# Turning the adaLN blocks of the pair steps by transpositions, and making some of them two slots earlier

## The reference

```
mod = silu(c) @ w_ada + b_ada          # 9 conditioning rows (1 prompt, 8 samples), 6144 columns
shift1, scale1, gate1, shift2, scale2, gate2 = split(mod, 6)
h = rms_norm(x, g_norm1) * (1 + scale1) + shift1
qa, ka, va, qb, kb, vb, qi, ki, wi, fl, ga, gb = split(h @ w_in)
oa = sparse_attend(...)   # top 128 keys of the indexer's scores, ALiBi, QK-norm
ob = forget_attend(...)   # causal, with cumulative log forget values, QK-norm
x = x + gate1 * ((sigmoid(ga) * (oa @ w_o_a) + sigmoid(gb) * (ob @ w_o_b)) @ w_out)
h2 = rms_norm(x, g_norm2) * (1 + scale2) + shift2
x = x + gate2 * (square(relu(h2 @ w_up)) @ w_down)
```

## Time and profile before

| | us |
|---|---|
| median of 3 runs | 942.34 |
| lowest, highest | 941.03, 943.38 |
| the profiled execution | 939.24 |
| its span | 937.4 |
| TensorE busy in the span | 919.6 (98%) |
| VectorE busy | 493.9 (53%) |
| ScalarE busy | 396.2 (42%) |

### The profile page before, as it was taken

One profiled execution on the slowest core, in us unless ns is written; L12 is line 12 of the kernel. 1 busy time (PEld: TensorE's weight loads), 2 busy tenths in 40 slices (PEclk: granted clock), 3 DMA queues, 4 the chain that ended last, 5 costly groups with the idle time before them and its releaser, 6 DMA issues.

```text
span 937.4 us, 19878 instructions
## 1 busy us (share of the span) xinstructions
PE 919.6 (98%) x7554; PEld 847.5 (90%) x7554; DVE 493.9 (53%) x1178; ACT 396.2 (42%) x829; POOL 141.0 (15%) x140
## 2 busy tenths in 40 slices
PE   8999999999999999999999999999999999999997
PEld 7797678777878878998999999999999999999997
DVE  3654778864645797731277576444333344443332
ACT  3354646654756667233334244333111244431121
POOL 4200233232236674300000000000000000000000
PEclk9999999999999999999999999999999999999999
DMA  9648765256325554977233431233333333333312
GB/s 319 219 117 235 188 214 174 71 169 193 110 64 158 163 183 131 279 251 249 69 91 97 129 90 47 69 92 94 98 96 91 90 90 89 89 89 90 89 45 92
DMA packets 176233, 124.54 MB, mean 133 GB/s; under 512 B 14739, under 2 KB 152019, under 8 KB 176164
## 3 DMA queue, kind: packets, MB, share of 16 engines
q1 hardware_dynamic: 176034, 123.50, 43.6%
q10 hardware_dynamic: 130, 0.10, 0.0%
HBM read 116.99 MB, written 6.59 MB: 132 GB/s over the span
## 4 chain that ended last, share of the span: by engine, by line
PE 88%; DVE 5%; issue 4%; ACT 2%; POOL 1%; POOLq 0%; ACTq 0%; DVEq 0%
PE bank L976 24%; PE bank L977 23%; PE bank L978 23%; PE bank L1064 2%; PE bank L1087 2%; PE bank L1043 2%; PE bank L882 2%; PE bank L1073 2%; PE bank L1105 1%; PE bank L1261 1%; PE bank L900 1%; PE bank L1049 1%; PE bank L1128 1%; DVE sel L2027 1%; PE bank L1118 1%
## 5 line engine op out<-in xcount | busy, mean ns | idle before, releaser
L976 PE MATMUL bank<-h_hi,w_hi 128*128 128x256 f32 (+1 forms) x1232 | 357.5, 290 | 1.2 <-issue 0.6
L977 PE MATMUL bank<-h_lo,w_hi 128*128 128x256 f32 (+1 forms) x1232 | 348.0, 282 | 0.0
L978 PE MATMUL bank<-h_hi,w_lo 128*128 128x256 f32 (+1 forms) x1232 | 347.5, 282 | 0.0
L976 PEld LDWEIGHTS bank<-h_hi,w_hi 128*128 128x128 f32 x1232 | 232.3, 189 | 23.5 <-issue 17.0
L977 PEld LDWEIGHTS bank<-h_lo,w_hi 128*128 128x128 f32 x1232 | 232.1, 188 | 0.0
L978 PEld LDWEIGHTS bank<-h_hi,w_lo 128*128 128x128 f32 x1232 | 231.7, 188 | 0.0
L976 PE MATMUL bank<-u_hi,w_hi 128*128 128x264 f32 (+1 forms) x512 | 145.1, 283 | 0.0
L977 PE MATMUL bank<-u_lo,w_hi 128*128 128x264 f32 (+1 forms) x512 | 144.7, 283 | 0.0
L978 PE MATMUL bank<-u_hi,w_lo 128*128 128x264 f32 (+1 forms) x512 | 144.5, 282 | 0.0
L2444 DVE TENSOR_TENSOR w_lo<-raw,w_hi 128x1024 fp32r<-128x1024 f32 x58 | 71.1, 1225 | 132.9 <-ACT w_hi L1783 132.9
L1783 ACT ACTIVATE w_hi<-raw 128x1024 fp32r<-128x1024 f32 x58 | 61.3, 1056 | 139.8 <-PE bank L978 139.8
(11 more groups left out here) (330 smaller groups left out, 1372.2 us busy)
## 6 DMA issues: line engine op xcount, KB each, us to landing
raw<-in_w_in SPq DMA_DIRECT2D x44, 512.0 KB, 4.0
part<-in_w_ada SPq DMA_DIRECT2D x32, 512.0 KB, 5.5
raw<-in_w_up SPq DMA_DIRECT2D x32, 512.0 KB, 4.1
raw<-in_w_down SPq DMA_DIRECT2D x32, 512.0 KB, 4.0
ada<-in_w_ada SPq DMA_DIRECT2D x4, 2048.0 KB, 13.6
kv<-in_cache_k_b SPq DMA_DIRECT2D x16, 256.0 KB, 4.1
qbc<-q_d SPq DMA_DIRECT2D x16, 256.0 KB, 4.6
kv<-in_cache_k_a SPq DMA_DIRECT2D x16, 256.0 KB, 4.5
```

The source lines that it names most:

```text
L976: mm(out, hi[:, k, :], x_h, start=first and k == ks[0], stop=False)
L977: mm(out, hi[:, k, :], x_l, start=False, stop=False)
L978: end = mm(out, lo[:, k, :], x_h, start=False, stop=last and k == ks[-1])
```

## The change

A block is turned by four plain transpositions of 128x128 against `ident`, each into its own 128 columns of bank 3. VectorE sums the four groups of 32 with one reduction into a new tile `mod_sum`, waits for it, and adds the bias from there. `fold_p` and its copy on GpSimd go; `cond_kept` is now signalled by the copy of `cond_p`. In steps 2, 3 and 5 the two halves of the block stand in slots 0 and 1 (before: 2 and 3), so that the turn stands at the end of slot 1 and the sum at the start of VectorE's slot 2. Steps 0, 1 and 4 keep their slots. There, in slot 4, `to_features` of the queries comes behind `turn_probs`, `scores` and the indexer's scores; in steps 2, 3 and 5 it stays ahead of them. `load_part` follows `ADA_AT`. The new tile takes 576 bytes a partition, and the tiles behind it move up by that much.

```diff
--- before.py
+++ after.py
@@ -61,7 +61,7 @@
 SPL = 2
 ADA_BLOCKS = 4
 ADA_ORDER = [0, 2, 1, 3] + list(range(4, 12))
-ADA_AT = [(p, s) for p in range(6) for s in range(0 if p in (1, 4) else 2, 4)]
+ADA_AT = [(p, s) for p in range(6) for s in (range(4) if p in (1, 4) else (0, 1) if p else (2, 3))]
 N_H = NCH + 2
 KEPT = list(range(T_WO + NCH + SPL, T_MLP)) + [T_MLP + 2, T_MLP + 3]
 N_KEPT = NCH - SPL
@@ -185,6 +185,7 @@
         rs8 = new("rs8", [P, 8])
         neghalf = new("neghalf", [P, 8])
         sm_tok_s = new("sm_tok_s", [NS, P])
+        mod_sum = new("mod_sum", [P, 4, 9])
         page_row = new("page_row", [1, NS * NPAGE], I32)
 
         x_t = new("x_t", [P, NCH, T])
@@ -302,7 +303,6 @@
         rs_all = sb("rs_all", [P, T], F32, h_hi_at + 4 * T * 4)[0]
         mod_row, _, e1 = sb("mod_row", [P, 2, SEQ], F32, ts_at)
         cond_p, _, e2 = sb("cond_p", [P, NCH, 32], F32, ts_at + 2048)
-        fold_p, _, e2 = sb("fold_p", [P, 9], F32, e2)
         assert e2 <= e1
         part = [sb(f"part{j}", [P, 2, SEQ], F32, at)[0] for j, at in enumerate((pad_at, padb_at, padb_at + 4096, e1))]
         nrm0, _, e1 = sb("nrm0", [P, 2, SEQ], F32, e1)
@@ -819,8 +819,7 @@
             pool.wait_ge(gq_consts, 1)
             pool.wait_ge(h_hi_ready, N_H)
             pool.wait_ge(h_lo_ready, N_H)
-            pool.tensor_copy(cond_p[:, :, :], cond_t[:, :, :])
-            pool.tensor_copy(fold_p[:, :], fold[:, :]).then_inc(cond_kept, 1)
+            pool.tensor_copy(cond_p[:, :, :], cond_t[:, :, :]).then_inc(cond_kept, 1)
 
             def power(n):
                 pool.wait_ge(ms_tok, n + 1)
@@ -1046,7 +1045,7 @@
             def mod_turn_part(n):
                 pe.wait_ge(mod_row_ready, ADA_BLOCKS + n + 1)
                 for q in range(4):
-                    last = mm(bank[3][:, 9 * q:9 * q + 9], mod_row[:, 0, q * P:(q + 1) * P], fold_p[:, :], start=True, stop=True)
+                    last = tr(bank[3][:, q * P:(q + 1) * P], mod_row[:, 0, q * P:(q + 1) * P], ident[:, :])
                 last.then_inc(mod_turned, 1)
 
             def unit(U):
@@ -1194,7 +1193,8 @@
                         to_tokens(p, 0)
                     if s == 4:
                         to_tokens(p, 1)
-                        to_features(p, 0)
+                        if (p, 3) not in ADA_AT:
+                            to_features(p, 0)
                     if s == K_BACK:
                         to_features(p, 1)
                 if s == 0 and 1 <= p <= N_PAIRS:
@@ -1215,6 +1215,8 @@
                     values(U - 5)
                 if (p, s) == slot_before(*SIDE[4]):
                     first_samples(p)
+                if s == 4 and (p, 3) in ADA_AT:
+                    to_features(p, 0)
                 if (p, s) in SIDE:
                     side_step(SIDE.index((p, s)))
                 if (p, s) in ADA_AT[1::2]:
@@ -1899,7 +1901,9 @@
             def mod_add_part(n):
                 at = slice(4 * ADA_ORDER[ADA_BLOCKS + n], 4 * ADA_ORDER[ADA_BLOCKS + n] + 4)
                 dve.wait_ge(mod_turned, ADA_BLOCKS + n + 1)
-                dve.tensor_tensor(mod_t[:, at, :], bank[3][:, 0:36].rearrange("p (q c) -> p q c", c=9),
+                link(dve.tensor_reduce(mod_sum[:, :, :], bank[3][:, :].rearrange("p (q j c) -> p q c j", q=4, j=4)[:, :, 0:9, :],
+                                       AX_X, ALU.add))
+                dve.tensor_tensor(mod_t[:, at, :], mod_sum[:, :, :],
                                   vec_t[:, at].unsqueeze(2).to_broadcast([P, 4, 9]), ALU.add).then_inc(mod_ready, 1)
 
             def rest_h(src, j, value):
```

## The result

The changed kernel took 944.91 us (median of 20 runs, 941.68 to 946.34) beside 942.13 us for the kernel before (20 runs, 938.72 to 945.32): ratio 1.0029, 95% interval 1.0019 to 1.0039. It is 2.8 us slower; the prediction said 1.5 us faster, 940.8, with 938.0 to 943.0 as the range.

What follows compares the result with a forecast made beforehand. TensorE, busy 98% of the span, was taken as the bound, with VectorE nearly a second one in step 2. Gains and losses over pair steps 0 to 5 summed to -1.5 us, giving 940.8 us; eight in ten: 938.0 to 943.0.

Steps and rivals of the forecast that it cites:

- Step 0: Pair step 0: the turn is 0.5 us shorter, but waits for `tok` use up the lead; 0 gained.
- Step 2: Pair step 2: new `ki_pt` wait +1.2, turn -0.5, late VectorE +0.8; together 1.5 us lost.
- the wait for `ki_pt`: Step 2, slot 0: the moved block's first products wait for ScalarE's copy before writing bank 3; 1.2 us lost.
- the lateness of VectorE: Step 2: with less TensorE work as cover, VectorE's sum for slot 4 and `tok` for slot 6 come 0.8 us late.
- Step 3: Pair step 3: `ki_pt` wait +0.4, wait for probabilities covered -0.8, turn -0.5 us.
- Step 4: Pair step 4: two shorter turns with no wait near; 1.0 us gained.
- Step 5: Pair step 5: one shorter turn, bank 3's reader done by then; 0.5 us gained.
- step 1: Pair step 1: first turn's 0.5 lost waiting for `w_ada`; second turn 0.5 and late queries 0.1 give 0.6 us gained.
- rival (b): VectorE's scaling of the mean squares is stretched beside GpSimd's `w_lo` in steps 2 and 3: +1.6, 943.9 us; chance 0.08.
- Rival (d): TensorE's clock falls to 1.2 GHz behind the eight turns: +24 us, 965 us; chance 0.01.
- Rival (a): Every turned block's 0.5 us reaches the end: -4.0, 938.3 us; chance 0.30 with its mixture at -3.
- Rival (c): Transpositions take the old turn's 0.92 us, so turns gain nothing: +1.5, 943.8 us; chance 0.04.

Runs made afterwards that it cites:

- the guard: VectorE's scaling of the mean squares in the form that also writes its accumulator; alone on the kernel before: 939.90 us, ratio 0.9977.
- e6: Changed kernel with the sums written to PSUM and the scaling of the mean squares also writing its accumulator: 939.43 us, ratio 0.9972 to before.
- e2: Changed kernel with the sums written to unused columns of PSUM bank 3 in place of SBUF: 943.85 us, ratio 1.0018 to before.
- e3: New turn alone on the kernel before, sums in SBUF, blocks and queries left in their old places: 945.05 us, ratio 1.0035.
- e5: New turn alone on the kernel before, blocks and queries in their old places, sums in PSUM: 941.88 us, ratio 0.9993.
- e7: New turn alone on the kernel before, sums in PSUM, scaling of the mean squares also writing its accumulator: 938.72 us, ratio 0.9960.
- P3: Third of four profiles taken of each of the two compared kernels, with no edit, to see where the clock falls; no total time given.

## Why the prediction was wrong

**The terms.** Step 0: 0 forecast, -0.3 measured; late queries give it. Step 2: the wait for `ki_pt` 1.2 forecast, 1.34 measured; the lateness of VectorE 0.8 forecast, 0.95 measured at the sum of squares. Step 3: -0.9 forecast, -0.57 measured; the waits for `ki_pt` (0.50) and probabilities (gone) came as forecast, and 0.28 us for `tok` behind a scaling of 1.30 us beside `w_lo` is the rest. Step 4: -1.0, measured -1.10. Step 5: -0.5 forecast, -0.14 measured; the turn gives it, a later side step (0.50 us of idleness for 0.15) takes 0.35 back, and it goes with the guard (e6: -0.50).

**The step that failed** is what was said of step 1: "Lead 0.6 us", a gain. Measured +0.5 to +2.7, a loss, in four profiles. The text priced what the change adds on VectorE as a reduction and took the add as it was. But the edit moved the add's first operand from PSUM to SBUF, and the add of step 1 stands beside `w_lo`: 1.78 us for 0.20 (shown by e2 and, at twice the price, by e3), and TensorE waits 1.06 us for it. With the add and the scaling out of the way of `w_lo` (e6) step 1 gives -0.30, half of the forecast. The part of `w_ada` in slot 2 was read rightly as a wait that eats the first turn's gain, but not as one that varies from run to run: from none listed to 1.73 us in the changed kernel.

**The second** is step 2: +1.5 forecast, +2.7 measured. Of the 1.2 us missing, some 0.3 are the two forecast waits coming out longer, and 0.9 the scaling beside `w_lo` (4.97 us from the sum to `tok` for 4.11; 3.96 with the guard). It was rival (b), at 0.08 and 943.9 us. The prediction judged that `w_lo` would end 1 us ahead of the sum of squares; it ended 1.2 us behind it, 171.56 against 170.32. Rival (b) puts the steps at +1.6, and +0.9 to +1.6 are measured in three of four profiles; the mechanism deserved far more than 0.08 once VectorE was forecast 0.8 us late in just that place. Its price was not right either: 1.9 us for step 2 and 1.2 for step 3, where 0.9 and 0.3 were lost, and it did not have the add of step 1.

**The rest is the clock.** Of the 2.8 us, the steps make 0.9 to 1.6 in three of four profiles. The half-clock stretch near 341 us, which four profiles of the changed kernel have and four of before have not, is worth 1.6; 0.2 to 0.4 come later. That makes 2.7 to 3.6 between profiles. It agrees roughly with the runs: mean clock 0.995 in 20 of the changed kernel, 0.997 in 35 of before, which by 0.85 us for each 0.001 is an estimate of 2.0 us, by 0.45 one of 1.0. Rival (d) named the clock, but with the wrong cause and price: not turns, at 24 us for all eight, but waits, at 1.6 us each. And the wait near 341 us is no work of the change, since the kernel before has it as well: the change moved it in time, from a moment at which the four profiles of before go free to one at which the clock falls. That part of the loss is bad luck as far as a forecast from this trace can go; why those moments and not others stays open.

Rival (a) is excluded by e5 and e7: even without the add and the moves, the turns give 1.6 to 2.0 us, not 4. Rival (c) is excluded by the 0.42 us of the turn.

## What to carry over

When an edit puts a small VectorE operand in SBUF that was in PSUM, look for what GpSimd runs beside it: the instruction lasts until GpSimd's ends, and keeping one operand in PSUM costs nothing (0.20 us beside `w_lo`, as without it). A block of TensorE work moved ahead is also cover taken away from where it stood; ask which queue was just in time there. A wait of 2 us on TensorE can cost 1.6 us more in clock, so the long waits are worth closing even where they look small: the guard on one instruction of 8 elements gave 1.8 us in the kernel before (941.73 to 939.90). And a difference of one such stretch between two profiles says little of the change: compare several profiles of each kernel, and the clocks of the runs.

## What the hardware showed

- A `tensor_scalar` from SBUF to SBUF on 8 elements and a `tensor_tensor` with two SBUF operands on 36 last until GpSimd's `w_lo` ends (0.56 to 2.25 us for 0.17 to 0.20); reductions from SBUF (0.67 to 0.69 us) beside the same `w_lo`, the add with one operand in PSUM and the accumulating form of `tensor_scalar` don't.
- A half-clock stretch lasts some 3.4 us, once twice that, and costs TensorE 1.6 us. In the 20 profiles each one begins within 2 us behind a wait of 1.4 us or more, but not every such wait has one (the 1.73 us for a part of `w_ada` and the 1.99 us for `tok` in the changed kernel's P3 have none), and none follows a wait of 0.7 to 1.34 us. The one at 22 to 25 us goes with the opening: in all 15 profiles whose first 20 products took 6.5 us or more it is there, in the five with 6.42 or less it isn't. The wait of 1.40 us ahead of it is the same in all 20; counted from where TensorE goes to full pace, it begins at 14.0 to 15.3 us in the 15 and at 15.4 to 15.8 in the five. That is a property of the execution, not of the kernel (before has it in one of four profiles), and puts the index scores at 75.5 to 76.8 us in place of 73.3 to 73.7.
